# A decoder step on one core: residual loads in quarters, operand jobs and setup jobs moved by slots, four banks for the first transposes

## The chip, the cores and the metric

The kernel runs on one core of a Trainium2 chip. The metric is the device time of one execution in microseconds; the kernel before takes 1031.95 us (median of three runs, 1031.47 to 1033.26).

## What is computed

One step of a hybrid decoder layer, all in fp32: a prompt of 512 tokens and 8 decode samples go through the same weights. Cut to what matters here:

```python
hp = rms_norm(yp, g_norm)                          # 512 x 2048
z = einsum('bsd,de->bse', hp, w_in)                # one projection, 2048 x 7168
od = diff_attn_prompt(...); ow = dilated_prompt(...)
mk, mv = memory_kv(mem_prompt, g_mem, w_mem_kv)    # rms_norm of 256 memory tokens, then 2048 x 1024
om = memory_attn(qm, mk, mv)
cat = concat([rms_norm(od, g_sub) * silu(gd), ow * silu(gw), om * silu(gm)])
yp = yp + einsum('bse,ed->bsd', cat, w_out)        # 2048 x 2048, residual add
y_prompt = rms_norm(yp, g_final)
```

The samples do the same with cached keys and values. Keys and values are outputs too.

## The kernel before

The work is cut into slots, and every engine runs the same list of slots in its own program order; semaphores alone hold the engines together. A slot has one piece of weight work on PE, a `quarter`: four 128x128 weight blocks times 520 columns (256 for the memory tokens). Each product is made of three matmuls, of a high and a low half of both factors: hi·hi, hi·lo, lo·hi. ACT rounds a weight quarter to its high half (`split_hi`, L1342) and DVE subtracts to get the low one (`split_lo`, L1668), three slots ahead of PE, in a ring of four. SP loads the raw weights into a ring of eight; in SP's program order a load waits for the split (`s_lo`) or sum (`s_sum`) that frees its place, and later loads stand behind it.

**Slots.** Slots 0 to 31 are the eight memory tiles (mk, mv), 32 to 255 the input projection, with attention and the decode samples put between, `IN_END` = 256 on the output projection. Output tiles 0 and 1 are plain (8 slots), tiles 2 to 13 go in six pairs of 14 slots, with seven products instead of eight, whose operands on the weight side are sums (S1 to S4, `weight_sum`, slots 0, 1, 1, 2 and 4 to 7 of the pair) and on the activation side T1 to T4. Pairs start at `IN_END` + 8, 22, 36, 50, 64 and 78. Tiles 14 and 15 are plain again. `plan()` puts jobs into slots; within a slot a rank orders them, and jobs of equal rank keep the order in which they were put.

**Startup.** PE transposes the memory tokens in eight `prep` steps of four 128x128 transposes into `s_ps`, two banks in turn, so prep u waits for the low half (`prep_lo`, DVE, `s_plo`) of prep u - 2. ACT (`prep_hi`) and DVE (`prep_lo`) work in the order of u, and the first five weight splits stand after preps 0, 1, 2, 4 and 6 (`FIRST_SPLITS`). PE's order is prep 0 to 3, quarter 0, prep 4, 5, quarter 1, prep 6, 7, quarter 2, quarter 3. Quarter r of the first tile needs the low halves of the first 2r + 2 preps. `z` holds two tensors of two banks; the first two tiles use bank 0 of each, the third and fourth bank 1.

**Setup jobs.** The memory tokens' norm is put onto the memory tiles when they leave PSUM: `memory_rstd` (slot 9) scales an identity by the two token factors on DVE (`r_diag`, L2058), PE multiplies it with ones (L1261), DVE copies it to `r_mem`. Prompt tokens get `squares` on ACT (L1320, slots 9, 12, 14, 18), `token_rstd` on POOL and `scale_tokens` on DVE (L1611, a slot after). A memory tile leaves PSUM in its `evac` (DVE, slots 10 and 11 for tiles 0 and 1, 12 for tile 2) and is turned to token order in `nat` (PE into `t_ps`, copied by ACT at L1431 into `k_nat`, stored by SP; slots 11, 13 and 14).

**Output operand.** The gated heads `cat` are split into `act_hi` (ACT, L1588) and `act_lo` (DVE, L2136), four of 16 blocks in each of the slots `IN_END` - 3 to `IN_END`; block 15 needs the gate of the last memory head. Tile 0's quarter r waits for 4r + 4 blocks (`s_clo`). T1 to T4 are made by eight `operand_add` jobs on DVE (four instructions each, L1737 to L1742, `T_ADDS`) and eight `operand_hi`/`operand_lo` jobs (`T_SPLITS`, L1421 on ACT, L1749 on DVE).

**Residual.** The residual x goes into `nat`, the place of `cat`, once all operands are made: in slot `IN_END` + 3, SP waits for the adds and for block 15 and issues four loads of 1 MB (512 columns of all 512 tokens each). Output tile e is turned by PE (`ynat`), and DVE adds it (`y_add`, L2007), waiting for load e // 4. Tiles 4, 8 and 12 are turned in slots `IN_END` + 39, + 67 and + 91.

**SP's order in a slot.** First the weight loads that are due (`LOADS[loaded][5] <= s`), then pages, stores, and last the residual. Of each pair's eight weight loads the last two are due in the tenth and eleventh slot of the pair before: for the third pair after the first, in `IN_END` + 46 and + 47; for the sixth, in + 74 and + 75; for the second, in + 18 and + 19.

Of the kernel before, what the change touches and what calls it, by code (L numbers as in the profile page):

```python
# [31 lines left out]
P = 128  # L32
D_MODEL = 2048
KT = D_MODEL // P
# [15 lines left out]
WIN_RING = 8  # L50
SPLIT_RING = 4
AHEAD = 3
FIRST_SPLITS = (0, 1, 2, 4, 6)
SOFT_AT = (0, 3, 5, 7, 8)
LATE_KEYS = (1, 2)
PAGE_RING = 6
# [69 lines left out]
FIRST_IN = AT["qd", 0, 0]  # L126
FIRST_OUT = AT["y", 0, 0]
N_PREP = KT // 2
# [25 lines left out]
OPS, START, DONE, PAIRS_OF_TILES = [], [], {}, []  # L154
# [119 lines left out]
def Y_NAT_AT(n):  # L274

    e = TILES[n][1]
    if e < FIRST_PAIRED:
        return IN_END + (11, 16)[e]
    if UNIT_OF[n] not in PAIR_AT:
        return DONE[n] + 1  # L280
    if e > LAST_PAIRED - 2:
        return DONE[n] + (3 if e % 2 else 1)
    return DONE[n] + (9 if e % 2 else 5)


T_ADDS = ((2, -11), (0, -10), (1, -9), (4, -8), (5, -7), (3, -4), (6, -2), (7, 1))
T_SPLITS = ((2, 0), (1, 0), (2, 1), (1, 1), (3, 0), (3, 1), (4, 0), (4, 1))
T_SPLIT_AT = (-4, -3, 2, 2, 3, 4, 6, 8)
T_ADDED = tuple(1 + max(j for j, (kt, _) in enumerate(T_ADDS) if kt // 4 <= half) for half in range(2))


def plan():
# [6 lines left out]
    def put(s, kind, what=None, cost=0.0, pe=0.0):  # L299
        slots[s].append((kind, what))  # L300
        load[s] += cost
        span[s] += pe
# [5 lines left out]
    for u in range(N_PREP):  # L308
        put(16 + 3 * u // 2, "prep", (1, u), 0.7)
    put(5, "mem", "squares")  # L310
    put(9, "mem", "rstd")
    put(11, "consts")
    put(20, "lambda")
    for k, s in enumerate((6, 7, 11, 25)):
# [3 lines left out]
    for n, (kind, h, c) in enumerate(TILES):  # L318
        s = DONE[n]
        if UNIT_OF[n] not in PAIR_AT:  # L320
            put(s + (6, 3)[n] if n < 2 else s, "evac", n, 0.65 if kind in ("gd", "gw") else 1.3 if kind == "gm" else 0.0)
        if kind in ("mk", "mv", "kd", "kw", "vd", "vw"):
            put(s + (7, 5)[n] if n < 2 else s + (2 if n < FIRST_IN else 1), "nat", n)
        if kind == "y":
            put(Y_NAT_AT(n), "ynat", n, 0.8)
            put(Y_NAT_AT(n) + (2 if c == 0 else 0), "ysq", n)
            if (h, c) == (KT - 1, 1):
                put(s + 2, "mean", 0)
                for k in range(2 * (NBLK - HEAD)):
                    put(s + 3 + 2 * k // (4 - HEAD), "norm", (HEAD + k // 2, k % 2))  # L330
                for k, later in enumerate((2, 3, 6, 8)):
                    put(s + later, "ys", k)
# [192 lines left out]
def hybrid_decoder(nc, x_prompt, x_sample, mem_prompt, cache_k_diff, cache_v_diff, page_table, cache_k_win,  # L525
# [4 lines left out]
    with ExitStack() as ctx:  # L530
# [287 lines left out]
        def _(sp):  # L818
# [88 lines left out]
            def slot(s, jobs):  # L907
# [32 lines left out]
                for kind, what, use in (PLAN[s - 1] if s else []):  # L940
# [25 lines left out]
                    if kind == "kvrows":  # L966
                        sp.wait_ge(s_tfree, use["tb"] + 1)
                        row = 0
                        for dst, nt in out_rows[what]:
                            for t in range(nt):  # L970
                                sp.dma_start(dst[:, t * P:(t + 1) * P], rows[row:row + DB, what, :]).then_inc(s_kvout[what], 16)
                                row += DB
                if s == IN_END + 3:
                    sp.wait_ge(s_tadd, len(T_ADDS))
                    sp.wait_ge(s_clo, KT)
                    for i in range(4):
                        cols = slice(512 * i, 512 * (i + 1))
                        sp.dma_start(nat[:, :, cols], x_t.rearrange("t p f -> p t f")[:, :, cols]).then_inc(s_res[i], 16)
                if s == IN_END - 10:
                    sp.wait_ge(s_mvout, 16 * H)  # L980
                    sp.wait_ge(s_ofull, USE["C", LAST_STEP["mem", H - 1]]["ob"] + 1)
# [19 lines left out]
        def prep_base(pair):  # L1001
            return pair * N_PREP

        @block.tensor
        def _(pe):
            def prep(pair, u):

                use = prep_base(pair) + u
                if pair:
                    pe.wait_ge(s_scaled, 2 * pair)  # L1010
                else:
                    pe.wait_ge(s_mtok[u // 2], 16)
                if use >= 2:
                    pe.wait_ge(s_plo, use - 1)
                first = 2 if pair == 1 else 0
                for k in range(2):
                    for t in range(2):
                        kt = 2 * u + k
                        last = nc.tensor.transpose(s_ps[:, use % 2, (2 * k + t) * P:(2 * k + t + 1) * P],
                                                   nat[:, first + t, kt * P:(kt + 1) * P], ident[:, :])  # L1020
                last.then_inc(s_pfull, 1)

# [281 lines left out]
        def _(act):  # L1304
# [17 lines left out]
            def prep_hi(pair, u):  # L1322
                use = prep_base(pair) + u
                g = gmn if pair == 0 else gn
                act.wait_ge(s_pfull, use + 1)
                if pair == 2:
                    act.wait_ge(s_quarter, IN_START - 3 + u // 2)
                first = N_MEM if pair == 1 else 0
                for k in range(2):
                    kt = 2 * u + k  # L1330
                    last = nc.scalar.activation(act_hi[:, kt, first:first + 2 * P], s_ps[:, use % 2, k * 2 * P:(k + 1) * 2 * P],
                                                ACT.Identity, scale=g[:, kt:kt + 1])
                last.then_inc(s_phi, 1)

# [165 lines left out]
            def slot(s, jobs):  # L1500
                if 2 <= s < N_SPLITS - AHEAD:
                    split_hi(s + AHEAD)
                for kind, what, use in jobs:
# [62 lines left out]
                    elif kind == "ysq":  # L1566
                        e = TILES[what][1]
                        act.wait_ge(s_tfree, USE["ynat", what]["tb"] + 1)
                        for k, i in enumerate(Y_BLOCKS[TILES[what][2]]):
# [4 lines left out]
                            else:  # L1574
                                act.wait_ge(s_kvout[0], 16 * 12)
                            nc.scalar.activation(rows[:, 0, :], nat[:, i, e * P:(e + 1) * P], ACT.Square,
                                                 scale=D_MODEL ** -0.5, accum_out=y_ss[:, i, e:e + 1]).then_inc(s_ysq, 1)
                if IN_END - 3 <= s <= IN_END:
                    if s == IN_END - 3:
                        act.wait_ge(s_tfree, USE["D", LAST_STEP["diff", 3]]["tb"] + 1)  # L1580
                        act.wait_ge(s_ofree, USE["C", LAST_STEP["dil", 3]]["ob"] + 1)
                        act.wait_ge(s_fin, 3)
                    r = s - (IN_END - 3)
                    act.wait_ge(s_quarter, IN_END - 3 + r)
                    for kt in range(4 * r, 4 * r + 4):
                        if kt >= 3 * H:
                            act.wait_ge(s_gated, kt - 3 * H + 1)
                        nc.scalar.activation(act_hi[:, kt, :], cat_t[:, kt, :], ACT.Copy).then_inc(s_chi, 1)  # L1588
# [10 lines left out]
        def _(dve):  # L1599
# [13 lines left out]
            def prep_lo(pair, u):  # L1613
                use = prep_base(pair) + u
                g = gmn if pair == 0 else gn
                dve.wait_ge(s_phi, use + 1)
                first = N_MEM if pair == 1 else 0
                for k in range(2):
                    kt = 2 * u + k
                    cols = slice(first, first + 2 * P)  # L1620
                    last = nc.vector.scalar_tensor_tensor(act_lo[:, kt, cols], s_ps[:, use % 2, k * 2 * P:(k + 1) * 2 * P],
                                                          g[:, kt:kt + 1], act_hi[:, kt, cols].bitcast(F32), ALU.mult, ALU.subtract)
                last.then_inc(s_plo, 1)

# [451 lines left out]
            def slot(s, jobs):  # L2076
                if 2 <= s < N_SPLITS - AHEAD:
                    split_lo(s + AHEAD)
                for kind, what, use in jobs:
# [50 lines left out]
                        mean(what)  # L2130
                    elif kind == "norm":
                        norm(*what)
                if IN_END - 3 <= s <= IN_END:
                    for kt in range(4 * (s - IN_END + 3), 4 * (s - IN_END + 3) + 4):
                        dve.wait_ge(s_chi, kt + 1)
                        nc.vector.tensor_tensor(act_lo[:, kt, :], cat_t[:, kt, :], act_hi[:, kt, :].bitcast(F32),  # L2136
                                                ALU.subtract).then_inc(s_clo, 1)
# [117 lines left out]
```

## Time and profile before

| | |
|---|---|
| median of three runs | 1031.95 us |
| profiled execution | 1031.1 us |
| its span, first to last instruction | 1029.3 us |
| mean granted TensorE clock | 0.996 |
| PE / DVE / ACT / POOL busy | 97% / 71% / 43% / 5% |
| DMA queue of SP, share of 16 engines' span | 65.3% |

PE is what to read: its idle time, and who ends it. The other engines' idle time counts only where PE waits for them. Times in timelines are microseconds from the span's start.

### The profile page before, as it was taken

What the parts mean: (1) busy time and instruction counts of PE and PEld (TensorE: products, weight loads), DVE (VectorE), ACT (ScalarE), POOL (GpSimd) and SP (SyncE); (2) the same over time, 40 slices, a digit from 0 to 9 for tenths busy, and PEclk for the clock granted to TensorE, in tenths of its full rate; (3) what the DMA queues carried; (4) which work ended last, traced back from release to release, by engine and by line L of the source; (5) the groups of instructions that cost most, each with busy time, mean ns of one, the idle gap of its engine ahead of it and who ended that gap; (6) DMA issues with size and microseconds to landing.
All of it is one profiled execution on the core that took longest, in us unless ns stands there. A gap on an engine that the chain in (4) does not pass through costs nothing. (4 is left out here: it accounts for less than half of the span.)

```text
span 1029.3 us, 24065 instructions
## 1 busy us (share of the span) xinstructions
PE 1001.1 (97%) x8079; PEld 979.1 (95%) x8079; DVE 735.3 (71%) x2708; ACT 444.6 (43%) x1174; POOL 54.2 (5%) x122
## 2 busy tenths in 40 slices
PE   6999999999999999999999999999999999999995
PEld 6999999999999999999999999999999999999995
DVE  5783267777888777778777667577774697788874
ACT  5763222223333333444433544225665365555552
POOL 0200000000000000000000000000001000000002
PEclk9999999999999999999999999999999999999998
DMA  9863289987978877776775686997753325433224
GB/s 298 247 195 107 64 265 255 290 288 218 271 223 248 266 238 222 219 229 200 235 217 171 191 262 173 250 284 245 213 167 106 116 71 195 122 104 104 83 83 166
DMA packets 254521, 203.31 MB, mean 198 GB/s; under 512 B 12481, under 2 KB 207671, under 8 KB 253751
## 3 DMA queue, kind: packets, MB, share of 16 engines
q1 hardware_dynamic: 253934, 200.67, 65.3%
q8 instruction: 64, 1.05, 0.4%
q10 hardware_dynamic: 464, 1.12, 0.3%
q14 instruction: 59, 0.48, 0.2%
HBM read 189.98 MB, written 11.76 MB: 196 GB/s over the span
## 5 line engine op out<-in xcount | busy, mean ns | idle before, releaser
L1088 PE MATMUL z<-act_hi,w_hi 128*128 128x260 f32 (+1 forms) x1984 | 428.9, 292 | 2.5 <-DVE act_lo L2136 2.0
L1088 PE MATMUL z<-act_hi,w_lo 128*128 128x260 f32 (+1 forms) x1984 | 410.1, 283 | 0.0
L1088 PE MATMUL z<-act_lo,w_hi 128*128 128x260 f32 (+1 forms) x1984 | 409.4, 283 | 0.0
L1088 PEld LDWEIGHTS z<-act_hi,w_hi 128*128 128x128 f32 x1984 | 312.3, 189 | 7.9 <-issue 5.4
L1088 PEld LDWEIGHTS z<-act_lo,w_hi 128*128 128x128 f32 x1984 | 310.7, 189 | 0.0
L1088 PEld LDWEIGHTS z<-act_hi,w_lo 128*128 128x128 f32 x1984 | 310.3, 189 | 0.0
L1668 DVE TENSOR_TENSOR w_lo<-w_raw,w_hi 128x512 fp32r<-128x512 f32 x300 | 205.8, 688 | 120.6 <-ACT w_hi L1342 119.5
L1342 ACT ACTIVATE w_hi<-w_raw 128x512 fp32r<-128x512 f32 x300 | 185.3, 625 | 189.3 <-PE z L1088 162.1
L1857 DVE CUSTOM_DVE_ANT_0 pages<-pages,q_bc 128x128 f32<-128x128 f32 x640 | 144.3, 286 | 24.7 <-DMA pages<-in_cache_k_win_dram 12.7
L1886 DVE SCALAR_TENSOR_TENSOR v_acc<-pages,dec_a,v_acc 128x256 f32<-128x256 f32 x224 | 94.3, 477 | 2.2 <-DMA pages<-in_cache_v_diff_dram 2.1
L1464 ACT ACTIVATE probs<-probs,st_n 128x128 f32<-128x128 f32 (+3 forms) x48 | 26.8, 558 | 79.9 <-DVE st_n L1796 79.5
L1114 PE MATMUL z<-t_hi,w_hi 128*128 128x260 f32 x192 | 55.3, 288 | 1.1 <-DVE w_lo L1668 1.1
L1114 PE MATMUL z<-t_hi,w_lo 128*128 128x260 f32 x192 | 54.2, 283 | 0.0
L1114 PE MATMUL z<-t_lo,w_hi 128*128 128x260 f32 x192 | 54.2, 282 | 0.0
L1857 DVE DVE_READ_ACCUMULATOR2_ANT dec_s<- 128x1 f32 x640 | 52.3, 82 | 0.0
L1342 ACT ACTIVATE w_hi<-w_sum 128x512 fp32r<-128x512 f32 x48 | 30.2, 630 | 41.9 <-DVE w_sum L1692 15.7
L1482 ACT ACTIVATE probs_T<-t_ps 128x512 f32<-128x512 f32 (+3 forms) x40 | 18.8, 469 | 68.2 <-PE t_ps L1174 55.9
L1789 DVE CUSTOM_DVE_ANT_0 probs<-s_ps,bias 128x128 f32<-128x128 f32 (+3 forms) x48 | 22.3, 489 | 35.8 <-PE s_ps L1147 22.7
L1668 DVE TENSOR_TENSOR w_lo<-w_sum,w_hi 128x512 fp32r<-128x512 f32 x48 | 33.0, 687 | 16.8 <-ACT w_hi L1342 16.8
L1114 PE MATMUL z<-act_hi,w_hi 128*128 128x260 f32 x144 | 41.5, 288 | 2.1 <-DVE w_lo L1668 2.1
L1114 PE MATMUL z<-act_lo,w_hi 128*128 128x260 f32 x144 | 40.7, 283 | 0.0
L1114 PE MATMUL z<-act_hi,w_lo 128*128 128x260 f32 x144 | 40.7, 283 | 0.0
(232 smaller groups left out, 1161.7 us busy)
## 6 DMA issues: line engine op xcount, KB each, us to landing
w_raw<-in_w_in_dram SPq DMA_DIRECT2D x224, 256.0 KB, 4.4
pages<-in_cache_k_diff_dram SPq DMA_DIRECT2D x128, 256.0 KB, 4.9
pages<-in_cache_v_diff_dram SPq DMA_DIRECT2D x128, 256.0 KB, 3.5
w_raw<-in_w_out_dram SPq DMA_DIRECT2D x64, 256.0 KB, 2.8
w_raw<-in_w_mem_kv_dram SPq DMA_DIRECT2D x32, 256.0 KB, 6.2
cat<-in_x_prompt_dram SPq DMA_DIRECT2D x8, 1024.0 KB, 7.8
q_bc<-q_rows_dram SPq DMA_DIRECT2D x32, 256.0 KB, 6.6
pages<-in_cache_mem_k_dram SPq DMA_DIRECT2D x16, 256.0 KB, 6.8
```

The source lines that it names most:

```text
L1088: last = nc.tensor.matmul(zb[:, bank, 0:b - a], lhs[:, w], rhs[:, kt, a:b], start=(kt == 0 and m == 0), stop=(kt == KT - 1 and m == 2))
L1114: last = nc.tensor.matmul(out, lhs[:, w], rhs[:, j, :], start=(i == 0 and j == 0 and m == 0), stop=(i == 1 and j == 3 and m == 2))
L1342: nc.scalar.activation(hi, raw, ACT.Copy).then_inc(s_hi, 1)
L1464: last = nc.scalar.activation(probs[:, c, 0:w], src, ACT.Exp, bias=st_n[:, t % 2, c:c + 1], scale=SCALE, accum_out=st_l[:, t % 2, c:c + 1])
L1482: nc.scalar.activation(probs_T[:, 0:w], t_ps[:, 0:w], ACT.Copy).then_inc(s_tfree, 1)
L1668: nc.vector.tensor_tensor(lo, raw, hi.bitcast(F32), ALU.subtract).then_inc(s_lo, 1)
L1789: last = nc.vector.tensor_tensor_reduce(probs[:, c, 0:w], s_ps[:, c, 0:w], bias[:, bi % 2, SEQ - w:SEQ], 1.0, LOWEST, ALU.add, ALU.max, st ...
L1857: last = nc.vector.tensor_tensor_reduce(seg, seg, q_bc[:, i % 2, k * P:(k + 1) * P], 1.0, 0.0, ALU.mult, ALU.add, s3[:, t, col:col + 1])
L1886: last = nc.vector.scalar_tensor_tensor(acc[:, seg], pages[:, slot, seg], a, acc[:, seg], ALU.mult, ALU.add)
```

## The change

Seven edits, all in the order and place of work; what is computed stays the same.

- The residual's four loads go out in slots `IN_END` + 3, + 20, + 46 and + 74, the first with the old waits, the others with none.
- Operand add 6 moves from slot -2 to +1 (counted from `IN_END`), ahead of add 7; operand split 1 (counted from 0) moves from -3 to +2, split 3 from +2 to +3, split 4 from +3 to +4 (`T_SPLIT_AT`).
- Block 15 of the output operand is split in slot +1, behind that slot's other jobs, the rest as before.
- The first eight preps use four banks, two of `s_ps` and bank 1 of both `z`, and wait for the low half of prep u - 4.
- The first weight splits stand after preps 0, 2, 4, 6 and 7.
- `memory_rstd` moves from slot 9 to 10, the evacuations of tiles 0 and 1 to 11 and 12, their turning to 12 and 14.
- Output tile 12 is turned a slot later (`DONE` + 2).

```diff
-FIRST_SPLITS = (0, 1, 2, 4, 6)
+FIRST_SPLITS = (0, 2, 4, 6, 7)
...
     if e > LAST_PAIRED - 2:
-        return DONE[n] + (3 if e % 2 else 1)
+        return DONE[n] + (3 if e % 2 else 2)
...
-T_ADDS = ((2, -11), (0, -10), (1, -9), (4, -8), (5, -7), (3, -4), (6, -2), (7, 1))
+T_ADDS = ((2, -11), (0, -10), (1, -9), (4, -8), (5, -7), (3, -4), (6, 1), (7, 1))
...
-T_SPLIT_AT = (-4, -3, 2, 2, 3, 4, 6, 8)
+T_SPLIT_AT = (-4, 2, 2, 3, 4, 4, 6, 8)
+HEADS_AT = ((0, 1, 2, 3), (4, 5, 6, 7), (8, 9, 10, 11), (12, 13, 14), (15,))
+RESIDUAL_AT = (3, 20, 46, 74)
...
-    put(9, "mem", "rstd")
+    put(10, "mem", "rstd")
...
-            put(s + (6, 3)[n] if n < 2 else s, "evac", n, 0.65 if kind in ("gd", "gw") else 1.3 if kind == "gm" else 0.0)
+            put(s + (7, 4)[n] if n < 2 else s, "evac", n, 0.65 if kind in ("gd", "gw") else 1.3 if kind == "gm" else 0.0)
...
-            put(s + (7, 5)[n] if n < 2 else s + (2 if n < FIRST_IN else 1), "nat", n)
+            put(s + (8, 6)[n] if n < 2 else s + (2 if n < FIRST_IN else 1), "nat", n)
...
-                if s == IN_END + 3:
-                    sp.wait_ge(s_tadd, len(T_ADDS))
-                    sp.wait_ge(s_clo, KT)
-                    for i in range(4):
-                        cols = slice(512 * i, 512 * (i + 1))
-                        sp.dma_start(nat[:, :, cols], x_t.rearrange("t p f -> p t f")[:, :, cols]).then_inc(s_res[i], 16)
+                if s - IN_END in RESIDUAL_AT:
+                    i = RESIDUAL_AT.index(s - IN_END)
+                    if i == 0:
+                        sp.wait_ge(s_tadd, len(T_ADDS))
+                        sp.wait_ge(s_clo, KT)
+                    cols = slice(512 * i, 512 * (i + 1))
+                    sp.dma_start(nat[:, :, cols], x_t.rearrange("t p f -> p t f")[:, :, cols]).then_inc(s_res[i], 16)
...
+        def prep_bank(use):
+
+            if use < N_PREP:
+                return (s_ps[:, 0, :], s_ps[:, 1, :], z[0][:, 1, :], z[1][:, 1, :])[use % 4]
+            return s_ps[:, use % 2, :]
...
-                if use >= 2:
-                    pe.wait_ge(s_plo, use - 1)
+                if use >= (4 if use < N_PREP else 2):
+                    pe.wait_ge(s_plo, use - (3 if use < N_PREP else 1))
...
-                if IN_END - 3 <= s <= IN_END:
+                if IN_END - 3 <= s <= IN_END + 1:
...
-                    r = s - (IN_END - 3)
-                    act.wait_ge(s_quarter, IN_END - 3 + r)
-                    for kt in range(4 * r, 4 * r + 4):
+                    act.wait_ge(s_quarter, min(s, IN_END))
+                    for kt in HEADS_AT[s - (IN_END - 3)]:
...
-                if IN_END - 3 <= s <= IN_END:
-                    for kt in range(4 * (s - IN_END + 3), 4 * (s - IN_END + 3) + 4):
+                if IN_END - 3 <= s <= IN_END + 1:
+                    for kt in HEADS_AT[s - (IN_END - 3)]:
```

The transposes' target and the two reads of it (`prep`, `prep_hi`, `prep_lo`) go through `prep_bank`.

## Rows read from the trace of the kernel before

**Rows 1.** Page, busy share; then PE's waits: total, times, longest, in us.
```profile
PE 1001.1 (97%) x8079; PEld 979.1 (95%) x8079; DVE 735.3 (71%) x2708; ACT 444.6 (43%) x1174; POOL 54.2 (5%) x122
...
PE z L1114 <- DVE w_lo L1668: 3.2, 5, 1.4
PE s_ps L1019 <- DVE act_lo L1621: 2.4, 4, 1.1
PE z L1088 <- DVE act_lo L2136: 2.0, 2, 1.3
...
PE t_ps L1134 <- DVE tall L1719: 0.8, 1, 0.8
```

**Rows 2.** Timeline of the startup; then groups of PE, 10.96-13.6 and 14.9-16.4.
```profile
10.22 1.09 PE L1019 MATMUL s_ps<-ident,cat 128*128 128x128 f32 x4 [0.30 <-DVE act_lo L1621]
...
10.96 0.56 PE L1088 MATMUL z<-act_hi,w_hi 128*128 128x256 f32 x1
...
15.56 0.88 DVE L1621 SCALAR_TENSOR_TENSOR act_lo<-s_ps,gmn,act_hi 128x256 fp32r<-128x256 f32 x2 [2.46 <-ACT act_hi L1331]
...
20.53 0.36 PE L1088 MATMUL z<-act_hi,w_hi 128*128 128x256 f32 x1 [0.49 <-DVE act_lo L1621]
...
L1088 PE MATMUL z<-act_lo,w_hi 128*128 128x256 f32 x4 | 1.7, 416 | 0.0
...
L1088 PE MATMUL z<-act_lo,w_hi 128*128 128x256 f32 x4 | 1.1, 280 | 0.0
```

**Rows 3.** Timeline around slots 9 and 10.
```profile
31.20 1.89 ACT L1320 ACTIVATE gate<-cat 128x2048 f32<-128x2048 f32 x1
...
32.01 0.48 DVE L2058 TENSOR_SCALAR r_diag<-ident,tok_r 128x128 f32<-128x128 f32 x2
...
32.54 0.70 PE L1261 MATMUL o_ps<-r_diag,ones 128*128 128x256 f32 x2 [0.55 <-DVE r_diag L2058]
...
33.81 0.69 DVE L1668 TENSOR_TENSOR w_lo<-w_raw,w_hi 128x512 fp32r<-128x512 f32 x1
...
34.75 1.28 DVE L1611 TENSOR_SCALAR cat<-cat,tok_r 128x2048 f32<-128x2048 f32 x1
```

**Rows 4.** Timeline of ACT around slot 14.
```profile
40.31 0.37 ACT L1431 ACTIVATE k_nat<-t_ps 128x256 f32<-128x256 f32 x1
...
41.09 1.92 ACT L1320 ACTIVATE gate<-cat 128x2048 f32<-128x2048 f32 x1
```

**Rows 5.** Timeline of DVE before the output projection.
```profile
830.70 1.24 DVE L1749 TENSOR_TENSOR t_lo<-t_raw,t_hi 128x1040 fp32r<-128x1040 f32 x1
...
834.90 0.42 DVE L1737 TENSOR_TENSOR t_raw<-cat 128x260 f32<-128x260 f32 x1
...
836.38 2.52 DVE L2136 TENSOR_TENSOR act_lo<-cat,act_hi 128x520 fp32r<-128x520 f32 x4
```

**Rows 6.** The residual's loads by source line, durations in ns; ACT's timeline behind them.
```profile
L978 SPq DMA_DIRECT2D cat<-in_x_prompt_dram x4: 507/620/907, 849.5 to 851.4; - x4
...
DMA to landing us min/median/max: 6.1/9.2/12.4
...
865.37 0.63 ACT L1342 ACTIVATE w_hi<-w_raw 128x512 fp32r<-128x512 f32 x1 [6.38 <-DMA w_raw<-in_w_out_dram]
```

**Rows 7.** The fourth pair: load due in +47, timeline, busy time 928.1 to 938.0.
```profile
L826 SPq DMA_DIRECT2D w_raw<-in_w_out_dram x1: 368/368/368, 927.4 to 927.4; - x1
...
DMA to landing us min/median/max: 2.7/2.7/2.7
...
930.11 0.63 ACT L1342 ACTIVATE w_hi<-w_raw 128x512 fp32r<-128x512 f32 x1 [0.91 <-DMA w_raw<-in_w_out_dram]
...
946.31 0.69 DVE L1668 TENSOR_TENSOR w_lo<-w_raw,w_hi 128x512 fp32r<-128x512 f32 x1
...
947.09 0.35 PE L1114 MATMUL z<-t_hi,w_hi 128*128 128x260 f32 x1
...
928.10:938.00 9.90, 9.90 (x85) 9.90 (x84) 9.90 (x19) 4.79 (x10) 1.16 (x2) 1.00 0.10 29
```

## What the change will do to the time

> **What bounds the kernel now.** I read the page's busy shares first, then the list of PE's waits, then the timeline at the places that the diff touches. PE is busy for 97% of the span, and it waits for few things [rows 1]; the waits that the change can reach sum to 2.4 (first transposes) + 2.0 (`act_lo` of the output's operand) + 3.2 (`w_lo` in the first pair) + 0.8 (turning tile 12) [rows 1] + 0.5 (`r_diag` [rows 3]) = 8.9 us. What the change can give is no more than that, plus what half-speed work at the start may lose. What it can cost has no such limit: PE runs its instructions in program order, so each wait put ahead of a quarter is lost in full. I therefore go through the slots one by one, engine by engine.
>
> **Startup (four banks, later splits).** Before, the third prep waits for the low half of the first, and the fourth until 10.22 for that of the second; quarter 0 follows at 10.96 [rows 2]. With four banks preps 2 and 3 run straight on, and quarter 0, which needs the first weight split and two low halves, starts at 10.22: 0.74 us sooner. From there the order on DVE decides: the four low halves of preps 4 to 7 and two weight splits (0.88 and 0.69 us each [rows 2, 3]) must end before quarter 3, which starts at 20.53 [rows 2]. The change alters which splits these are, not how many. The low half of prep 4 (15.56) comes about 0.6 us earlier; 0.14 of the 0.74 is lost because prep 4 then lies wholly at half speed. Half speed is plain in the same matmul: 416 ns early, the 1.2 GHz level, against 280 later, the 2.4 GHz one [rows 2]. So **-0.6 us**. The bounds: 0 if DVE's chain does not move, -2.0 if the fast clock also comes a stretch earlier (a rival, below). Writing into z's second banks is not in the trace; s_ps banks are the nearest rows, and I take the same duration. The weight loads on SP that wait for the moved splits are not later: those splits end before SP gets to these loads. PE's list has no wait for weights before the first pair [rows 1].
>
> **`rstd` one slot on.** Before, in slot 9 DVE does split 12, then the two `r_diag` scalings (32.01), and PE waits 0.55 us for them after quarter 9 [rows 3]. In slot 10 the put order of the planner stands (both jobs have rank 6): token scaling 2 comes first, `rstd` behind it. So on DVE `r_diag` is now queued behind split 13, which waits for ACT's split, which stands behind `squares` 2 (31.20, 1.89 us), and behind scaling 2 (1.28 us) [rows 3]. In times of before: split 13 at 33.81, scaling at 34.42, `r_diag` at 35.62, ready at 36.10 (0.48 us). PE, which was done with quarter 9 at 32.0 (32.54 less the wait) and has only quarter 10 more in hand (1.45 us for twelve matmuls, so free at 33.45), waits 2.65 us instead of 0.55: **+2.1 us**. Quarter 11, the constants' transpose and all that follows stand behind it; tile 0's evacuation, turning and store go a slot on with it and have two slots of cover. The bounds: +0.9 if only split 13 stood in front (ready 34.9), +2.7 if the 0.55 was hidden otherwise. The startup's gain moves both sides alike.
>
> **Natural copies of tiles 1 and 2.** Their slots were 13 and 14; now both are 14, and in that slot ACT does `squares` 4 (1.92 us) before the copies [rows 4]. PE turns tile 1, then must wait for ACT to empty `t_ps` before it turns tile 2. From quarter 13's end ACT needs the split (0.6), `squares` (1.9) and the copy (0.37): 3.0 us with gaps; PE gets there after quarter 14 and one transpose pair, 1.7 us. **+1.3 us**, bounds 0 and +1.9 (the squares alone). The copy of tile 2 then waits for the store of tile 1, with two slots of cover on PE.
>
> **Output operands.** DVE is the bound there: PE waits for `act_lo` twice, 2.0 us in all [rows 1]. Ahead of the last `act_lo` block the change removes the second operand split (1.24 us at 830.70), but puts in front of it operand add 7 (an add is four instructions; the one at 834.90 ends at 836.38, where the next block begins) and the weight split of slot +1 (0.69); add 6 stays ahead, only later. +1.48 + 0.69 - 1.24 = +0.93 us [rows 3, 5]. The earlier blocks come sooner and the first wait goes, but quarter 3 of tile 0 still needs block 15, so the two waits become one of about 2.9: **+0.9 us**, bounds 0 and +1.5. On SP the first residual load waits for the same two semaphores, and is released about 1 us sooner, by the earlier adds.
>
> **Residual, first quarter.** Before, four 1-MB loads go out from 849.5 to 851.4 and land 6.1 to 12.4 us after issue, 2.7 us apart ((12.4 + 1.9 - 6.1)/3); the two weight loads behind them on SP's queue come last, and ACT waits 6.38 us for one at 865.37 [rows 6]. PE's 3.2 us (five waits, all in this pair) follow from that one: two at once, three because DVE never catches up. With one quarter ahead the weights land some 5 us before they are wanted: **-3.2 us**, bounds -1.8 (only the first two waits go) and -3.2.
>
> **Residual, quarters 2 and 3.** This is where I part from what the edit seems to buy. Quarter 1 (slot +20) goes out behind all weight loads of its pair, and the queue is then idle for 10 us: free. Slots +46 and +74 are the tenth slot of a pair, and in SP's order the last weight load of the next pair (due in slots +47 and +75) comes *after* the residual. Before, that load is issued at 927.4 and lands 2.7 us later, and ACT is already waiting for it (0.91 us, to 930.11) [rows 7]. DVE has no room: it is busy for 9.90 of 9.90 us there (one of two such stretches) [rows 7], and its sums, splits and part adds are in order, so a late split moves the sums S3 and S4, on which the last four operands of the pair depend; these already arrive within 0.1 us of PE's need (the split of 946.31 ends at 947.00, PE starts on it at 947.09 [rows 7]). A 1-MB load issued at 926.3 lands at 932.4 if it takes the 6.1 us of the first one of before, and the weight load 0.8 later: 933.2 instead of 930.1, 3.1 us late. With 0.1 to 0.2 us of slack and a little for an easier queue I take 2.75 us each: **+5.5 us**, bounds 0 (nothing behind it is delayed) and +6.2. From below the rows give 1.2 us of delay: 2.7 us of transfer, less the 1.5 us between the two issues. The Trainium skill (DMA: Bandwidth & Descriptors, Queues, rings and completion order) says that SP's loads share one ring on each DMA engine and are taken in ring order, which speaks against these two slots. Its fit in Anatomy of one DMA, 2.0 us + bytes/436 GB/s, gives 4.4 us for 1 MB where the row has 6.1; by it, as an estimate, the load would be only some 1.2 us late and the term +2.0.
>
> **Tile 12 a slot later.** PE does quarter 0 of tile 14 first, and the 0.8 us behind C12 goes [rows 1]; the weights for that quarter are split just before it. POOL's add and ACT's squares of the tile go a slot on too, two slots before anything needs them. **-0.8 us**, bounds -0.8 and 0. The end of the kernel follows PE as before.
>
> **Sum.** -0.6 + 2.1 + 1.3 + 0.9 - 3.2 + 5.5 - 0.8 = +5.2 us. The profiled execution took 1031.1 us (span 1029.3), so 1036.3; the median of the runs, 1031.95, is 0.85 above it, which gives **1037.2 us**.
>
> **Rivals.** (a) *The residual quarters hide.* If a weight load behind a residual quarter is no later than before, both pairs keep their time and the sum is -0.3: 1031.7, not slower. The place is slots +47 and +75, the point from which it decides is a landing within 0.15 us of today's 2.7. Against it: the two loads behind the four residual loads landed last [rows 6]. Chance 0.11. (b) *They hide in part*, 1.2 us late each, as the transfer alone or the skill's fit would have it: +2.0 instead of +5.5, 1033.7. Chance 0.12. (c) *The clock rises earlier.* With fewer gaps PE's work from 5.7 us on may bring the fast clock before quarter 0 instead of after it; that gives up to 1.4 us more, 1035.8. The Trainium skill (TensorE: Matmul & The Clock Gate, Part 1) says that the engine starts at half clock and sustained activity releases it; the 416 and 280 ns agree that it did so once here. Chance 0.2. (d) *The 2.65-us stall drops the clock* to half for some microseconds: about +2, 1039.2. PE's waits of before are at most 1.4 us once it runs [rows 1], so rows neither show nor exclude it. Chance 0.08. (e) *The slot moves cost nothing*, because the order within a slot is not what I read: 3.4 us less, 1033.8; chance 0.08. (f) (a) and (e) together: 1028.3, faster; chance 0.08. The forecast itself 0.33.
>
> **Chances.** About 0.2% (2.1 us) is what a measurement of this kernel tells from no change. Slower by more (above 1034.0): the forecast, (c), (d), and a part of (b) and (e) that lands above the bound, 0.33 + 0.2 + 0.08 + 0.1 = 0.71. Same: (a) and the rest of (b) and (e), 0.21. Faster: (f), 0.08. The range 1031.6 to 1040 leaves (f) out and takes in (a), (d) and the upper bounds of the pairs (+0.7).
>
> **What will show it.** The list of PE's waits after: `r_diag` near 2.6 instead of 0.5, a new wait of `t_ps` on ACT's `k_nat` near 1.3, `act_lo` (the line of the operand's low halves) near 2.9, `w_lo` in the first pair gone but `w_lo` in two later pairs (near 930 and 972 plus the shift) of some 2.7 each, behind ACT waits on a weight DMA of 3 to 4 us. If the late pairs show no wait, the queue term is wrong, and with it the sign; if `r_diag` stays at 0.5, I misread the order in the slot.

## The result and the profile after

The changed kernel takes **1038.57 us** (median of seven runs, 1034.63 to 1039.46), the kernel before 1031.95 in the same runs; the ratio is 1.0055, with a 95% interval of 1.0037 to 1.0072. It is slower, as forecast (1037.2). Five of the seven runs lie at 1038.47 to 1039.46 us with a mean granted clock of 0.991 or 0.992, two at 1034.63 and 1034.66 us with 0.995. The profiled execution is one of the five: it took 1038.86 us, its span is 1037.0 us against 1029.3, so 7.7 us are to be explained.

PE's waits in the changed kernel (total, times, longest, in us), which answer to [rows 1]:

```profile
PE z L1097 <- DVE act_lo L2144: 3.3, 1, 3.3
PE o_ps L1270 <- DVE r_diag L2066: 2.7, 1, 2.7
PE z L1123 <- DVE w_lo L1676: 2.6, 7, 0.5
...
PE t_ps L1143 <- ACT k_nat L1440: 1.4, 1, 1.4
```

`r_diag` went from 0.5 to 2.7, `k_nat` is new with 1.4, the two waits for the output's low halves became one of 3.3, tile 12's 0.8 (`tall`) is gone, and `w_lo` went from five waits in one pair to seven small ones. The list grew by under 3 us in all, though, and the span by 7.7. What the list doesn't hold is TensorE's clock. Busy time by stretch (us, then PE, PEld, DVE, ACT, POOL, then the granted clock as a share of 2.4 GHz, the DMA share and GB/s), in the changed kernel:

```profile
35.00:36.00 1.00, 0.21 (x1) 0.21 (x2) 0.73 (x3) 0.00 (x0) 0.00 (x0) 0.83 0.93 352
36.00:37.00 1.00, 1.00 (x3) 0.82 (x4) 0.00 (x0) 0.00 (x0) 0.00 (x0) 0.50 1.13 331
39.00:40.00 1.00, 1.00 (x8) 0.82 (x8) 0.14 (x2) 0.38 (x2) 0.00 (x0) 0.96 0.47 125
...
849.00:852.00 3.00, 0.00 (x0) 0.00 (x0) 2.93 (x9) 0.55 (x1) 0.00 (x0) 0.91 0.29 87
852.00:855.00 3.00, 2.82 (x13) 2.85 (x14) 3.00 (x5) 2.01 (x3) 0.00 (x0) 0.50 0.41 104
855.00:858.00 3.00, 3.00 (x16) 3.00 (x16) 1.69 (x2) 0.18 (x1) 0.00 (x0) 0.50 1.01 370
858.00:861.00 3.00, 3.00 (x26) 3.00 (x26) 1.76 (x2) 2.87 (x5) 0.29 (x1) 0.95 0.33 95
```

Twice the clock falls to 0.50, the 1.2 GHz level, and both times it falls at the end of one of the two long waits; PE then does 16 matmuls in 3 us where it does 26 later. The profile of the kernel before (mean 0.996) has no such stretch between its start and its last microseconds.

A ledger shows the sizes. PE runs the same 8079 matmuls in both kernels, so the start of one and the same matmul in both timelines gives the delay up to there; what is added between two of them belongs to the edit between them.

| the same matmul, before and after (us) | delay | added since the line above | of it waits in the list | forecast |
|---|---|---|---|---|
| 31.00, 30.64 (after the first quarters) | -0.36 | -0.36 | | -0.6 |
| 38.45, 41.61 (after `rstd`) | +3.16 | +3.52 | 2.72 - 0.55 = 2.17 | +2.1 |
| 44.99, 49.77 (after tiles 1 and 2 are turned) | +4.77 | +1.61 | 1.40 | +1.3 |
| 850.04, 858.46 (after block 15) | +8.42 | +3.65 | 3.33 - 2.0 = 1.3 | +0.9 |
| 884.94, 889.16 (in the first pair's end) | +4.22 | -4.20 | 0.3 - 3.2 = -2.9 | -3.2 |
| 973.99, 980.47 (after the fourth pair) | +6.48 | +2.26 | 1.2 | +2.75 |
| 990.05, 998.67 (after the sixth pair) | +8.62 | +2.14 | 1.1 | +2.75 |
| 996.00, 1003.74 (after tile 12 is turned) | +7.74 | -0.88 | -0.75 | -0.8 |

**Slot 10**, which answers to [rows 3], in the timeline of DVE and PE:

```profile
33.45 0.69 DVE L1676 TENSOR_TENSOR w_lo<-w_raw,w_hi 128x512 fp32r<-128x512 f32 x1 [1.72 <-ACT w_hi L1351]
34.06 1.28 DVE L1619 TENSOR_SCALAR cat<-cat,tok_r 128x2048 f32<-128x2048 f32 x1
35.26 0.48 DVE L2066 TENSOR_SCALAR r_diag<-ident,tok_r 128x128 f32<-128x128 f32 x2
...
35.79 1.22 PE L1270 MATMUL o_ps<-r_diag,ones 128*128 128x256 f32 x2 [2.72 <-DVE r_diag L2066]
```

The order is the forecast one: split 13 (itself 1.72 us late behind ACT), scaling 2, then `r_diag`. **Slot 14**, which answers to [rows 4], in the timeline of ACT and PE: the squares of 1.90 us stand ahead of the copy of tile 1, and PE waits 1.40.

```profile
43.71 1.90 ACT L1329 ACTIVATE gate<-cat 128x2048 f32<-128x2048 f32 x1
...
45.60 0.36 ACT L1440 ACTIVATE k_nat<-t_ps 128x256 f32<-128x256 f32 x1
...
46.11 0.41 PE L1143 MATMUL t_ps<-ident,mem_kv 128*128 128x128 f32 x2 [1.40 <-ACT k_nat L1440]
```

**Block 15**, which answers to [rows 5], in the timeline: two operand adds and a split lie between block 14 and block 15 on DVE, 3.6 us in all.

```profile
847.77 0.69 DVE L1676 TENSOR_TENSOR w_lo<-w_raw,w_hi 128x512 fp32r<-128x512 f32 x1
848.38 0.43 DVE L1745 TENSOR_TENSOR t_raw<-cat 128x260 f32<-128x260 f32 x1
...
851.34 0.69 DVE L2144 TENSOR_TENSOR act_lo<-cat,act_hi 128x520 fp32r<-128x520 f32 x1
...
852.18 0.77 PE L1097 MATMUL z<-act_hi,w_hi 128*128 128x260 f32 x2 [3.33 <-DVE act_lo L2144]
```

**Residual quarter 2**, which answers to [rows 7]: by source line, the residual's load and the weight load of slot +47 behind it (duration of the issue in ns, when; then us from issue to landing):

```profile
L981 SPq DMA_DIRECT2D cat<-in_x_prompt_dram x1: 509/509/509, 930.5 to 930.5; - x1
...
DMA to landing us min/median/max: 5.3/5.3/5.3
...
L828 SPq DMA_DIRECT2D w_raw<-in_w_out_dram x1: 367/367/367, 931.6 to 931.6; - x1
...
DMA to landing us min/median/max: 5.1/5.1/5.1
```

ACT's timeline behind it:

```profile
936.67 0.63 ACT L1351 ACTIVATE w_hi<-w_raw 128x512 fp32r<-128x512 f32 x1 [3.26 <-DMA w_raw<-in_w_out_dram]
```

The weight load lands 5.1 us after issue instead of 2.7, 0.9 behind the residual's, and ACT waits 3.26 us for it instead of 0.91. PE's waits of this pair add up to only 1.2 us, in three pieces of 0.50, 0.34 and 0.37, but the pair loses 2.26. The difference is what a wait costs beside its listed idle time. The last of the sixth pair's three, in PE's timeline:

```profile
995.62 0.29 PE L1123 MATMUL z<-act_lo,w_hi 128*128 128x260 f32 x1
995.75 0.29 PE L1123 MATMUL z<-act_hi,w_lo 128*128 128x260 f32 x1
996.37 0.39 PE L1123 MATMUL z<-act_hi,w_hi 128*128 128x260 f32 x1 [0.34 <-DVE w_lo L1676]
996.60 0.28 PE L1123 MATMUL z<-act_lo,w_hi 128*128 128x260 f32 x1
```

Matmuls start 0.12 to 0.13 us apart. Across the wait it is 0.62, and the one after comes 0.23 later, not 0.12: 0.50 + 0.11 = 0.61 us are lost for 0.34 in the list. This interruption thus costs 0.27 us more than its idle time, the overlap with the matmul before and behind it. At the same price for each, three waits more in the fourth pair make 1.2 + 0.8 = 2.0 of its 2.26; four fewer in the first pair make 2.9 + 1.1 = 4.0 of its 4.20.

### The profile page after: what moved, and what is told of

It is laid out like the page before. It is cut to its first block and busy times, and to the rows that moved or that the text cites. A ratio compares the mean times of both kernels' runs of the same rounds, so it can differ in the third digit from the quotient of the medians.

```text
span 1037.0 us, 24064 instructions
## 1 busy us (share of the span) xinstructions
PE 1006.0 (97%) x8079; PEld 984.2 (95%) x8079; DVE 735.2 (71%) x2708; ACT 444.4 (43%) x1174; POOL 54.4 (5%) x122
```

## The experiments

Theory: the ledger's terms are local and add up; the two long waits also cost the clock; the residual quarters are late-makers by their place on SP's queue. Each rival stands with its run. Times are medians; the ratio is that to the kernel before on the same chip (1031.95 us for the changed kernel, 1031.55 to 1031.59 for the others), with its interval.

| run | us | ratio |
|---|---|---|
| changed kernel | 1038.57 | 1.0055 (1.0037 to 1.0072) |
| e1 setup jobs back | 1032.81 | 1.0014 (1.0004 to 1.0024) |
| e2 adds, splits, block 15 back | 1034.87 | 1.0029 (1.0018 to 1.0041) |
| e3 residual at +47, +75 | 1033.26 | 1.0012 (1.0001 to 1.0023) |
| e4 all three | 1026.59 | 0.9953 (0.9937 to 0.997) |
| e5 block 15 back alone | 1032.01 | 1.0003 (0.9993 to 1.0013) |
| e6 e4 with e5's order | 1023.25 | 0.9919 (0.9902 to 0.9937) |
| e7 before, a longer wait in slot 9 | 1035.33 | 1.0035 (1.0023 to 1.0047) |
| e8 e4, quarters 2 and 3 at +46, +74 from ACT | 1026.77 | 0.9955 (0.994 to 0.9969) |
| e9 the same from POOL | 1033.35 | 1.0022 (1.0012 to 1.0031) |
| e10 before, the new start alone | 1031.51 | 1.0001 (0.9992 to 1.001) |
| e11 before, half as much wait as e7 | 1033.27 | 1.0017 (1.0008 to 1.0027) |

### e1: setup jobs back

```diff
-    put(10, "mem", "rstd")
+    put(9, "mem", "rstd")
-            put(s + (7, 4)[n] if n < 2 else s, "evac", ...
+            put(s + (6, 3)[n] if n < 2 else s, "evac", ...
-            put(s + (8, 6)[n] if n < 2 else ..., "nat", n)
+            put(s + (7, 5)[n] if n < 2 else ..., "nat", n)
```

> The changed kernel with memory_rstd back in slot 9, the evacuations of tiles 0 and 1 back in 10 and 11, their turning back in 11 and 13; all else as changed. Theory (the order on DVE and ACT in these slots makes two waits, and the long one also costs the clock): the wait for r_diag falls from 2.72 to about 0.5 us, the wait for k_nat of 1.41 us goes, TensorE's granted clock stays at 1.0 from 15 us on to the output projection, and the time is some 5.3 us lower (2.2 + 1.4 + 1.7 for 3.41 us at half clock), 1033.3. Rival (the clock falls because the earlier start of the first transposes brings a burst and a gap, not because of the wait): half clock near 35 us stays, and only 3.6 us come back, 1035.

1032.81 us: 1.3 above the kernel before instead of 6.6, so 5.4 less (5.3 expected). PE's waits:

```profile
PE o_ps L1270 <- DVE r_diag L2066: 0.6, 1, 0.6
PE t_ps L1143 <- ACT k_nat L1440: 0.2, 1, 0.2
```

Busy time by stretch, columns as above:

```profile
33.00:36.00 3.00, 3.00 (x25) 2.69 (x23) 2.89 (x6) 0.90 (x3) 0.46 (x1) 1.00 1.00 378
36.00:40.00 4.00, 4.00 (x35) 4.00 (x35) 1.91 (x8) 3.32 (x5) 2.46 (x4) 1.00 1.02 252
847.00:850.00 3.00, 2.87 (x14) 2.90 (x15) 3.00 (x4) 1.96 (x3) 0.00 (x0) 0.54 0.41 105
```

Both waits are back to small ones, the clock stays up at 33 to 40 us, and it still falls behind the wait for block 15, which e1 left in. The earlier start is in e1 too, so the rival that blamed it falls.

### e2: adds, splits and block 15 back

```diff
-... (3, -4), (6, 1), (7, 1))
+... (3, -4), (6, -2), (7, 1))
-T_SPLIT_AT = (-4, 2, 2, 3, 4, 4, 6, 8)
+T_SPLIT_AT = (-4, -3, 2, 2, 3, 4, 6, 8)
-HEADS_AT = (..., (12, 13, 14), (15,))
+HEADS_AT = (..., (12, 13, 14, 15), ())
```

> The changed kernel with operand add 6 back in slot -2, operand splits as before, and block 15 of the output operand back in slot 0; all else as changed. Theory (block 15 stands behind two operand adds and a split on DVE, and the 3.33-us wait for it costs the clock): two waits of 0.7 and 1.3 us for act_lo come back in place of one of 3.33, no half clock near 851 us, and the time is 1.3 us lower by the wait and some 3 us by the clock, 1034.3. Rival (half clock there comes from something else, for example the change in load of the DMA queue): the clock still falls near 850 us and only 1.3 us come back, 1037.3.

1034.87 us: 3.3 above the kernel before, so 3.3 less than the changed one, where 4.3 was expected (3.9 between the two profiled executions). In PE's list the two waits of before come back:

```profile
PE z L1097 <- DVE act_lo L2144: 2.0, 2, 1.3
```

By stretch, the clock falls only behind slot 10:

```profile
36.00:40.00 4.00, 4.00 (x23) 3.68 (x22) 1.86 (x8) 0.83 (x3) 0.01 (x1) 0.70 0.83 222
846.00:850.00 4.00, 3.48 (x29) 3.17 (x27) 3.97 (x8) 1.68 (x3) 0.00 (x0) 1.00 0.23 68
850.00:854.00 4.00, 3.22 (x27) 3.25 (x28) 3.43 (x9) 1.25 (x2) 0.00 (x0) 1.00 0.25 72
```

In these two profiles e1 and e2 are mirror images: each stretch at half clock goes with its own wait, and the other stays.

### e3: the residual one slot later

```diff
-RESIDUAL_AT = (3, 20, 46, 74)
+RESIDUAL_AT = (3, 20, 47, 75)
```

> The changed kernel with the third and fourth residual quarters issued one slot later (+47 and +75), which is behind the last weight load of the next pair instead of ahead of it; all else as changed. Theory (queue order: the weight load lies behind 1 MB on SP's queue): that load lands 2.7 to 2.9 us after issue again instead of 5.0, the six waits for w_lo near 938 to 952 and 982 to 996 go, and the time is 4.2 us lower, 1034.4. Rival (a 1-MB load delays whatever is under way by its bytes, wherever it stands): the lateness stays within 1 us of what it was and under 1 us comes back, 1037.6 or more.

1033.26 us: 1.7 above the kernel before, so 4.9 less, where 4.2 was expected. The weight load that was 5.1 us under way, by source line:

```profile
L828 SPq DMA_DIRECT2D w_raw<-in_w_out_dram x1: 368/368/368, 929.7 to 929.7; - x1
...
DMA to landing us min/median/max: 2.9/2.9/2.9
```

The only `w_lo` wait left in PE's list is the first pair's:

```profile
PE z L1123 <- DVE w_lo L1676: 0.3, 1, 0.3
```

So the two quarters cost about what the ledger says, 4.4, and a place one slot on is free. The rest need not be from this edit: in this profile the clock rose at 9 us (below), the delay when tile 2 is turned (41.39 us before) is 4.1 us where the changed kernel's is 4.7, and half clock behind block 15 cost 1.5 us instead of 2.7.

### e4: all three undone

The edits of e1, e2 and e3 together.

> The changed kernel with all three of these undone: setup jobs and block 15 as before, residual quarters at +3, +20, +47 and +75. What stays of the change is four banks, the order of the first weight splits, the residual in quarters and tile 12 a slot later. Theory (the terms add up): -0.3 (start) - 4.0 (first pair) - 0.8 (tile 12) = 5.1 us less than before the change, 1026.9. Rival (the gains of the first pair were slack won only because PE came late to it): under 2 us less than before, 1030 or more.

1026.59 us, against 1026.9 expected: the terms add up, and what is left of the change (first pair, tile 12) is a real gain of 5.0 us that the three other moves had covered.

### e5: block 15 alone

```diff
-HEADS_AT = (..., (12, 13, 14), (15,))
+HEADS_AT = (..., (12, 13, 14, 15), ())
```

> The changed kernel with block 15 of the output operand back in slot 0, ahead of the two operand adds that stay in slot +1; all else as changed. Theory (block 15's place behind the adds is what makes the 3.33-us wait, and moving the adds and the split away from the blocks is a gain): DVE ends block 15 near 848.5 us, before PE's need near 848.9, so no wait of PE for the operand's low halves is left, the clock stays up near 851 us, and the time is 3.3 + 3.05 + about 0.25 (restart) = 6.6 us lower than the changed kernel, 1032. Rival (the adds in slot +1 only move the wait to the next quarter or to the first residual load): a wait of 1 to 3 us shows up right behind, 1034 to 1036.

1032.01 us, 0.4 above the kernel before, so 6.2 less than the changed one (6.6 expected). Busy time by stretch around the blocks:

```profile
840.00:850.00 10.00, 10.00 (x86) 10.00 (x85) 9.89 (x20) 4.73 (x8) 0.00 (x0) 1.00 0.27 79
```

PE is busy without a gap: not even the 2.0 us of before are left. So moving the adds and the split away from the blocks is a good edit, and one block, put behind them instead of ahead, turned its gain (2.0 us and two interruptions, some 2.5) into a loss of 3.65, clock included.

This profile shows one thing more. e5 keeps the late `rstd`, and PE waits for `r_diag` again, but here the clock doesn't fall (PE's timeline, then busy time by stretch):

```profile
34.37 0.48 PE L1270 MATMUL o_ps<-r_diag,ones 128*128 128x256 f32 x1 [2.21 <-DVE r_diag L2066]
...
34.00:38.00 4.00, 3.63 (x27) 3.40 (x28) 2.66 (x10) 1.32 (x3) 0.50 (x1) 1.00 1.03 361
```

The profiled execution was the fastest of e5's ten (1029.91 us).

### e6: the good parts together

e4, with the operand adds and splits of the change and block 15 in slot 0.

> As e4_all_three_back, but operand adds and operand splits in the slots of the change, with block 15 in slot 0. Theory: against e4 the two waits for the operand's low halves (0.75 and 1.28 us and about 0.25 us of restart each) go, 2.5 us less: 1024.1. Rival (the adds, late, hold the first residual quarter and with it the first pair's weights): no gain, 1026.6 or more.

**1023.25 us**, 0.8% under the kernel before, and the fastest of all (1024.1 expected). In PE's list from 800 us on only two waits are left, 0.6 us for `rows` and 0.4 for `w_lo`, and in this profile the clock does not fall before the last microseconds.

### e7 and e11: a wait and nothing else

```diff
                 dve.wait_ge(s_rr, 1)
+                spare = v_nat[:, :, :, :].rearrange("p a b c -> p (a b c)")
+                nc.vector.tensor_tensor(spare, spare, spare, ALU.mult)
```

This is e7; e11 has `nc.vector.tensor_scalar(spare, spare, tok_r[:, 0:1], None, ALU.mult)` in its place.

> The kernel before with one more VectorE multiplication of 128x2048 numbers (about 2.4 us; its result is used nowhere) ahead of r_diag in slot 9; nothing else is moved. Theory (a wait of TensorE of this length by itself drops its clock): the wait for r_diag grows from 0.55 to about 2.95 us, the granted clock falls to half behind it for 3.4 us or more, and the time grows by 2.4 + 1.7 = 4.1 us, 1035.7. Rival (the half clock of the changed kernel came from its other edits): the clock stays at 1.0 and the time grows by 2.4 us alone, 1034.0.

> The kernel before with one more VectorE scaling of 128x2048 numbers (1.28 us; its result is used nowhere) ahead of r_diag in slot 9: the wait for r_diag grows to about 1.8 us. Theory (only the long waits of 2.7 and 3.3 us cost the clock; before, 1.4 us did not): the granted clock stays at 1.0 and the time grows by 1.3 us, 1032.9. Rival (any longer wait here costs the clock): half clock behind it, 1034.5 or more.

e7 takes 1035.33 us, 3.7 more than the kernel before (4.1 expected). PE's timeline:

```profile
34.34 0.75 PE L1261 MATMUL o_ps<-r_diag,ones 128*128 128x256 f32 x1 [2.75 <-DVE r_diag L2060]
```

Busy time by stretch behind it:

```profile
34.00:37.00 3.00, 2.66 (x10) 2.48 (x11) 1.73 (x6) 0.00 (x0) 0.67 (x1) 0.57 1.09 344
37.00:40.00 3.00, 3.00 (x21) 2.69 (x20) 1.82 (x3) 0.84 (x2) 0.00 (x0) 0.86 0.32 80
```

In the otherwise unchanged kernel, a wait of 2.75 us is enough: the clock falls behind it. Not in each execution, though: the runs lie between 1033.5 and 1036.2, the fastest of them at the time of the wait alone (mean clock 0.997), the slowest above it. e11 takes 1033.27 us, 1.7 more (1.3 expected; PE also waits 0.7 us for `k_nat` there). Its wait, in PE's timeline, is 1.75 us:

```profile
33.51 0.48 PE L1261 MATMUL o_ps<-r_diag,ones 128*128 128x256 f32 x1 [1.75 <-DVE r_diag L2061]
```

By stretch, no half clock follows it:

```profile
34.00:37.00 3.00, 3.00 (x26) 2.84 (x25) 2.67 (x5) 0.63 (x1) 0.00 (x0) 1.00 1.07 324
870.00:874.00 4.00, 4.00 (x22) 3.68 (x21) 4.00 (x7) 2.23 (x5) 0.00 (x0) 0.57 0.00 0
```

But in the same execution, as the last row shows, half clock came behind a wait of 1.8 us in the first pair. The traces of all thirteen kernels, one execution each, show how far the length goes once the clock has risen: all seven waits of 2.7 to 3.4 us were followed by half clock, two of three of 2.1 to 2.4 (e9 and e10, not e5), one of five of 1.6 to 1.9, and of the shorter ones a single wait of 0.92 us (e4). So a longer wait was followed by it more often, and its length alone does not decide. What does is left open.

### e8 and e9: the same quarters from another queue

Both are e4 with the quarters in slots +46 and +74 again. In e8 ACT issues them at the end of its slot. In e9 POOL does, released by the same semaphore value as SP's weight load of that slot:

```diff
+            def residual(i):
+                due = [load for load in range(len(LOADS)) if LOADS[load][5] == IN_END + RESIDUAL_AT[i]]
+                kind, value = LOADS[due[-1]][4]
...
+                pool.wait_ge(s_lo if kind == "lo" else s_sum, value)
+                cols = slice(512 * i, 512 * (i + 1))
+                nc.gpsimd.dma_start(nat[:, :, cols], x_t.rearrange("t p f -> p t f")[:, :, cols]).then_inc(s_res[i], 16)
```

> As e4_all_three_back, but the third and fourth residual quarters go out in slots +46 and +74 again, from ScalarE's queue instead of SyncE's. Theory (queue order: the weight load is late because it lies behind 1 MB on the same queue): the weight loads of slots +47 and +75 land 2.7 to 3.2 us after issue, PE does not wait for w_lo in these pairs, and the time is that of e4, 1026.6. Rival (the bytes themselves are what delays: both loads share the same 16 engines): the weight loads take 4 to 5 us again, each pair loses 1 to 2 us, 1029 to 1031.

> As e8_act_queue, but the third and fourth residual quarters go out from GpSimd's queue, released by the same semaphore value as the weight load of slot +46 (+74), so that they start some 1.5 us ahead of the weight load of slot +47 (+75), as in the changed kernel; in e8 the lead was 4.2 us and the test blunt. Theory (order on SyncE's own queue): the loads of +47 and +75 land 2.7 to 3.2 us after issue and the time is that of e4, 1026.6. Rival (1 MB holds the shared engines, whichever queue it comes from): they land some 0.8 us after the residual quarter again, 4.5 us or more after issue, PE waits three times a pair for w_lo, and the time is 3 to 4 us higher, 1030.

e8 takes 1026.77 us, the number of my theory, but ACT issued the quarter 4.2 us ahead of the weight load of slot +47, not 1.1, so the test was blunt. e9 was made to sharpen it and takes 1033.35 us, 6.8 more than e4 against the kernel before, where the rival had 3 to 4 and my theory nothing. The weight load of slot +47 in e9, and the residual quarter ahead of it on POOL's queue, by source line:

```profile
L2240 POOL DMA_DIRECT2D cat<-in_x_prompt_dram x1: 961/961/961, 922.2 to 922.2; - x1
...
DMA to landing us min/median/max: 6.7/6.7/6.7
...
L828 SPq DMA_DIRECT2D w_raw<-in_w_out_dram x1: 368/368/368, 923.1 to 923.1; - x1
...
DMA to landing us min/median/max: 6.2/6.2/6.2
```

From a queue that is not SP's the weight load is no less late; it lands at 929.3, 0.4 us behind the residual quarter (922.2 + 6.7 = 928.9), as in the changed kernel 0.9 behind. In PE's list of the two pairs (918 to 990 us):

```profile
PE z L1123 <- DVE w_lo L1676: 4.7, 4, 2.3
```

The loss is larger than the rival's because the weight loads are later still than in the changed kernel: 6.2 us here and 6.9 in the sixth pair, against 5.1 and 5.0. The fourth pair loses 3.4 us by it; in the sixth, which loses 4.1, half clock also follows the wait of 2.3 us (0.57 from 978 to 982 us).

My theory falls: the order on SP's queue is not needed. 1 MB that is under way when the weight load starts delays it, from SP's queue and from POOL's; in e8, with a long lead, most of it was through by then. The Trainium skill (DMA: Bandwidth & Descriptors, Queues, rings and completion order) says that each DMA engine takes turns between queues and drains a whole packet from one before it switches. How much of a load is one such packet no run shows; in e9 the weight load got almost no turn from 924 to 926.5 us, while most of the residual quarter went through. The queues of POOL (q0) and SP (q1) in that stretch (entries as the profile counts them, MB, share of 16 engines):

```profile
q0 software_dynamic: 177, 0.72, 78.0%
q1 hardware_dynamic: 16, 0.01, 1.2%
```

### e10: the start alone

```diff
-FIRST_SPLITS = (0, 1, 2, 4, 6)
+FIRST_SPLITS = (0, 2, 4, 6, 7)
...
+            return (s_ps[:, 0, :], s_ps[:, 1, :], z[0][:, 1, :], z[1][:, 1, :])[use % 4]
...
-                if use >= 2:
-                    pe.wait_ge(s_plo, use - 1)
+                if use >= (4 if use < N_PREP else 2):
+                    pe.wait_ge(s_plo, use - (3 if use < N_PREP else 1))
```

> The kernel before with only the four banks and the later first weight splits. Theory (the start gains little: the chain of low halves on DVE sets quarter 3): 0.3 to 0.7 us less where the clock rises near 14 to 15 us, up to 1.5 us less where it rises near 9 to 10 us as in the profiles of e3 to e6, of which a wait for the memory weights' loads behind it takes back about 1 us; in the median 0.3 to 0.9 us less, 1030.7 to 1031.3. Rival (the early rise is worth its whole 2 us): 1029.5 or less.

1031.51 us against 1031.56: no difference. Its profile keeps a gain of 0.45 us up to the first pair and loses it there: that pair waits for weights behind the residual's 4 MB, and PE, earlier, waits longer, 2.2 us at once where it was 1.4, with half clock behind it (0.58 from 867 to 871 us).

```profile
PE z L1120 <- DVE w_lo L1674: 3.2, 3, 2.2
```

What four banks can do is seen where the clock rises early, in the profiles of e3, e4, e5, e6 and e9 (five of the ten that have them). A matmul of 256 columns at 11.4 us takes 0.28 us in e6 and 0.41 in the changed kernel.

In e6 quarter 3 starts 2.7 us earlier than before, but at 31 us only 1.27 of it is left, since PE then waits 1.13 us for `w_lo`, behind the memory weights' loads. A wait of 1.46 us for `k_nat`, with the setup jobs back in their old slots, takes the rest: at 45 us e6 is 0.55 us later than the kernel before. So an early clock gains nothing that lasts here. In e4 such a wait for `w_lo`, of 0.92 us at 25.9, was even followed by half clock from 27.2 to 30.6.

## Why the prediction was right, and where its steps were not

Its sum, +5.2 us, stands against 7.7 in the profile and 6.6 in the medians: the sign and most places hold, and the nearness of the number is in part luck. Step by step:

- **`rstd`**: +2.1 forecast, 2.17 in the wait. The order on DVE, the cause and the size hold.
- **Tiles 1 and 2**: +1.3 against 1.4 in the wait and 1.6 in the ledger. Holds.
- **Output operands**: +0.93 against 0.93: the matmul that waits for block 15 started at 846.48 before and starts at 852.18 now, a delay of 5.70, less the 4.77 before the blocks. (The wait in the list is 3.33 where about 2.9 was forecast, in part because one interruption fewer brings PE there sooner.) Holds, and e5 shows that it was block 15's place alone. The other 2.72 of the 3.65 come behind it, at half clock.
- **The clock** is the step that failed. The sum kept it at full speed; rival (d) had a fall behind `r_diag` alone, at +2 and with a chance of 0.08, and nothing behind the 2.9-us wait for block 15, which I had forecast as well. It fell behind both: +1.35 (3.52 - 2.17) and +2.72, together 4.1 us. e1, e2 and e7 show that the long waits bring it; the 2.2 us of e5 without a fall show that a wait does not always. The two runs at 1034.6 us and a mean clock of 0.995 are 4.2 us under the profiled one, about what the two falls cost; no trace of them shows whether these are what they lack, but it would leave the change at +2.7 us at full clock, half of the forecast. The error lay in the chance: rows of before had no wait over 1.4 us once PE ran, so they spoke neither for nor against a fall behind 2.7.
- **First pair**: -3.2 against -4.2. Cause right; the term summed listed idle time and left out the 0.27 us of each interruption.
- **Residual quarters 2 and 3**: +5.5 against 4.4. Place, victim and sign hold, and rival (a), that they hide, falls with the 5.1 us and with e3. The mis-sized term is the lateness: I took 6.1 us for a 1-MB load; in these slots it landed after 5.3, so the weight load was 2.4 us late (5.1 against 2.7), not 3.1. Of that the pair lost 2.26, so DVE's lack of slack holds. The reason given, the order on SP's queue, is not needed for it (e9). The fit that the prediction set beside its row, 4.4 us for 1 MB, is stated by the Trainium skill (DMA: Bandwidth & Descriptors, Anatomy of one DMA) for loads that GpSimd issues; SP's took 5.3 us here, GpSimd's 6.7 and 7.4 in e9.
- **Start**: -0.6 against -0.36 in the profile (-0.62 in e10's), and nothing in the time (e10). Rival (c), the earlier clock, happens in half the profiles, though not in that of the changed kernel.
- **Tile 12**: -0.8 against -0.88.

The errors, +4.1 for the clock and +0.6 for start, `rstd` and tiles, against -1.0 for the first pair and -1.1 for the quarters, make up the 2.5 us between 5.2 and 7.7: the total came out near partly because the pair terms were off in the other direction, so that half of the missed clock was covered by luck.

## What to carry to other kernels

Move a job by a slot only after reading what stands ahead of it in the new slot on every engine in program order; three of the edits here lost more than they could give by one instruction that came to stand behind another. Price a long wait of TensorE twice: its idle time, and the half clock that can follow it. Put a large load where no small, urgent one starts within some microseconds behind it; another queue did not help here.

## What was not expected of the hardware

- Half clock followed all seven traced waits of 2.7 to 3.4 us, and some shorter ones (2.3 us in e9, 2.2 in e10, 1.8 in e11, 0.92 soon after the start in e4), but not 2.2 us in e5, 1.9 in e9 or the 1.75 in e11's slot 9. A stretch at half clock cost 1.35 and 2.72 us in the changed kernel, on top of waits that had grown by 2.17 and 1.3.
- An interruption of PE's stream of 260-column matmuls cost 0.27 us beyond the idle time that the list of waits shows, in the one that was read matmul by matmul; the same for each makes up most of what the pairs gain and lose.
- A 256-KB load that starts 0.9 to 1.1 us behind a 1-MB load lands 0.4 to 0.9 us after it, from the same queue and from POOL's (5.0 to 6.9 us instead of 2.7).
